# Four unread 64x64 products ahead of nine trains of matmuls in a two-block transformer on one core

## What is computed

```python
for l in range(DEPTH):                                   # DEPTH = 2
    h = rms_norm(x, norm_mix[l])
    if l < N_A:
        x = x + short_conv_mixer(h, conv_w_in[l], conv_w[l], conv_w_out[l])
    else:
        x = x + moba_attention(h, moba_w_q[j], moba_w_o[j], cos, sin, k_blk, v_blk, k_mean)
    x = x + mem_cross_attention(rms_norm(x, norm_mem[l]), rms_norm(mem, norm_memkv[l]),
                                mem_w_q[l], mem_w_kv[l], mem_w_o[l])
    x = x + swiglu(rms_norm(x, norm_ffn[l]), ffn_w_gu[l], ffn_w_down[l])
    if l == N_A - 1:
        k_blk, v_blk, k_mean = shared_kv(x, kv_norm, w_kv, cos, sin)
```

## Time and profile before

| what | value |
|---|---|
| median of 3 runs | 1797.46 us (1796.14 to 1797.94) |
| the profiled execution | 1793.09 us, its span 1791.3 us |
| busy share of the span | PE 89%, DVE 49%, ACT 37%, POOL 8% |
| chain that ended last | PE 62%, issue 28%, DVE 5%, ACT 3%, DMA 2% |
| matmuls of lines 422 to 424 | 1360 each, busy 379 us each line |

### The profile page before, as it was taken

One profiled execution on the slowest core, in us unless ns is written; L12 is line 12 of the kernel. 1 busy time (PEld: TensorE's weight loads), 2 busy tenths in 40 slices (PEclk: granted clock), 3 DMA queues, 4 the chain that ended last, 5 costly groups with the idle time before them and its releaser, 6 DMA issues.

```text
span 1791.3 us, 35143 instructions
## 1 busy us (share of the span) xinstructions
PE 1586.7 (89%) x14818; PEld 1313.8 (73%) x14818; DVE 869.1 (49%) x1231; ACT 665.6 (37%) x870; POOL 149.9 (8%) x188
## 2 busy tenths in 40 slices
PE   8999999999999999999999799799898676666677
PEld 8999899988979889988888699698884222222223
DVE  5865466646665555664667588956641000000001
ACT  5545355434544444533555744525431000000001
POOL 5900000000000000000105011131010000000000
PEclk9999999999999999999999899999998687786679
DMA  7755656765736657755453153002879999999997
GB/s 245 257 194 185 189 161 192 235 235 165 259 118 215 201 157 218 194 173 194 112 157 106 61 167 117 25 27 95 301 289 406 420 421 421 421 421 421 421 420 299
DMA packets 254141, 417.17 MB, mean 233 GB/s; under 512 B 15102, under 2 KB 215345, under 8 KB 229425
## 3 DMA queue, kind: packets, MB, share of 16 engines
q1 hardware_dynamic: 253825, 414.59, 64.8%
q10 hardware_dynamic: 176, 0.53, 0.1%
HBM read 414.04 MB, written 1.05 MB: 232 GB/s over the span
## 4 chain that ended last, share of the span: by engine, by line
PE 62%; issue 28%; DVE 5%; ACT 3%; DMA 2%; POOL 0%; DVEq 0%; SPq 0%; POOLq 0%; ACTq 0%
PE bank L422 8%; PE bank L423 8%; PE bank L424 8%; PE bank L438 4%; PE bank L439 4%; PE bank L440 4%; PE bank L1864 2%; PE bank L1063 2%; PE bank L1065 2%; PE bank L1064 2%; PE bank L747 2%; PE bank L839 1%; DMA w_raw<-in_ffn_w_gu_dram 1%; DVE cy L1413 1%; ACT w_hi L243 1%
## 5 line engine op out<-in xcount | busy, mean ns | idle before, releaser
L250 DVE TENSOR_TENSOR w_lo<-w_raw,w_hi 128x2048 fp32r<-128x2048 f32 (+2 forms) x178 | 401.8, 2260 | 252.9 <-ACT w_hi L243 252.8
L243 ACT ACTIVATE w_hi<-w_raw 128x2048 fp32r<-128x2048 f32 (+2 forms) x178 | 334.1, 1881 | 150.7 <-DMA w_raw<-in_ffn_w_down_dram 61.7
L422 PE MATMUL bank<-h_hi,w_hi 128*128 128x256 f32 x1168 | 325.5, 279 | 6.0 <-DVE h_lo L635 3.8
L424 PE MATMUL bank<-h_hi,w_lo 128*128 128x256 f32 x1168 | 324.6, 278 | 0.0
L423 PE MATMUL bank<-h_lo,w_hi 128*128 128x256 f32 x1168 | 324.5, 278 | 0.0
L2659 PE MATMUL bank<-w_exp,xeT 128*32 128x256 f32 x2048 | 172.2, 474 | 81.7 <-DMA w_exp<-in_w_up_dram 48.3
L422 PEld LDWEIGHTS bank<-h_hi,w_hi 128*128 128x128 f32 x1168 | 220.8, 189 | 7.4 <-issue 7.2
L424 PEld LDWEIGHTS bank<-h_hi,w_lo 128*128 128x128 f32 x1168 | 220.2, 189 | 0.0
L423 PEld LDWEIGHTS bank<-h_lo,w_hi 128*128 128x128 f32 x1168 | 220.1, 188 | 0.0
L2659 PEld LDWEIGHTS bank<-w_exp,xeT 128*32 128x32 f32 x2048 | 65.5, 128 | 182.7 <-DMA w_exp<-in_w_up_dram 83.9
L2659 PE MATMUL bank<-w_exp,hT 128*32 128x256 f32 x1024 | 97.1, 516 | 51.6 <-DMA w_exp<-in_w_down_dram 51.6
(11 more groups left out here) (537 smaller groups left out, 3102.1 us busy)
## 6 DMA issues: line engine op xcount, KB each, us to landing
w_exp<-in_w_gate_dram SPq DMA_DIRECT2D x64, 1024.0 KB, 27.0
w_exp<-in_w_up_dram SPq DMA_DIRECT2D x64, 1024.0 KB, 26.9
w_exp<-in_w_down_dram SPq DMA_DIRECT2D x64, 1024.0 KB, 27.0
w_raw<-in_ffn_w_gu_dram SPq DMA_DIRECT2D x88, 512.0 KB, 5.0
w_raw<-in_w_in_dram SPq DMA_DIRECT2D x54, 512.0 KB, 4.8
w_mod<-in_w_mod_dram SPq DMA_DIRECT2D x24, 1024.0 KB, 7.0
w_raw<-in_ffn_w_down_dram SPq DMA_DIRECT2D x44, 512.0 KB, 4.3
w_raw<-in_mem_w_kv_dram SPq DMA_DIRECT2D x32, 512.0 KB, 4.6
```

Of the source, the lines that this page charges most:

```text
L243: e.activation(whi[slot][:, 0:w], raw[slot][:, 0:w], ACT.Copy).then_inc(S["hi_ready"], 1)
L250: e.tensor_tensor(wlo[slot][:, 0:w], raw[slot][:, 0:w], whi[slot][:, 0:w].bitcast(F32), ALU.subtract).then_inc(S["lo_ready"], 1)
L422: e.matmul(dst, whi[slot][:, lo:hi_], bh[:, k, :], start=begin, stop=False)
L424: ins = e.matmul(dst, wlo[slot][:, lo:hi_], bh[:, k, :], start=False, stop=end)
```

## The change

`lead_in` writes four products of 64 x 64 by 64, two in the upper left and two in the lower right quarter of TensorE's array, from the identity into the bank that the train's chunk writes next. Nobody reads them: the chunk's first product starts that bank anew. `fm_chunk` gets a parameter `lead`, the number of the chunk ahead of which they stand. Seven calls set it, which makes nine trains, since two of the calls are made for both layers. It is chunk 0 for the last third of the conv input and the block-attention query, chunk 1 for the others.

```diff
+    def lead_in(e, dst):
+
+        for _ in range(2):
+            for a_ in (0, 64):
+                e.matmul(dst[a_:a_ + 64, 0:64], ident[a_:a_ + 64, a_:a_ + 64], ident[a_:a_ + 64, a_:a_ + 64],
+                         start=True, stop=True)
+
-    def fm_chunk(bh, bl, width=256, kts=KT):
+    def fm_chunk(bh, bl, width=256, kts=KT, lead=None):
 
         fs = width // P
 
         def chunk(e, c, u, slot):
             by_tile = st.tiles is not None
+            if isinstance(c, int) and c == lead:
+                lead_in(e, G[u])
...
-    gemm(4, cols(W), fm_chunk(h_hi, h_lo), act_chunk=copy_bc(0), ready=[th])
+    gemm(4, cols(W), fm_chunk(h_hi, h_lo, lead=1), act_chunk=copy_bc(0), ready=[th])
...
-    gemm(4, cols(W, first=2 * D), fm_chunk(h_hi, h_lo), dve_chunk=conv_chunk, dve_links=9,
+    gemm(4, cols(W, first=2 * D), fm_chunk(h_hi, h_lo, lead=0), dve_chunk=conv_chunk, dve_links=9,
          dve_ready=[t_bc, t_z0, t_vcol])
...
-    gemm(4, cols(A["mem_w_kv"][0]), fm_chunk(*h2), act_chunk=copy_fm(kT), ready=[t_memkv], act_ready=[t_conv_out],
+    gemm(4, cols(A["mem_w_kv"][0]), fm_chunk(*h2, lead=1), act_chunk=copy_fm(kT), ready=[t_memkv], act_ready=[t_conv_out],
...
-        gemm(4, cols(A["mem_w_q"][l]), fm_chunk(*into), act_chunk=copy_fm(qT), ready=[tx], act_ready=[tx],
+        gemm(4, cols(A["mem_w_q"][l]), fm_chunk(*into, lead=1), act_chunk=copy_fm(qT), ready=[tx], act_ready=[tx],
...
-        gemm(FT, source, fm_chunk(h_hi, h_lo), act_chunk=act_silu, dve_chunk=dve_gate, dve_links=2,
+        gemm(FT, source, fm_chunk(h_hi, h_lo, lead=1), act_chunk=act_silu, dve_chunk=dve_gate, dve_links=2,
...
-    gemm(4, cols(A["w_kv"]), fm_chunk(h_hi, h_lo), act_chunk=copy_fm(kT), ready=[th], act_ready=[th2])
+    gemm(4, cols(A["w_kv"]), fm_chunk(h_hi, h_lo, lead=1), act_chunk=copy_fm(kT), ready=[th], act_ready=[th2])
...
-    gemm(4, cols(A["moba_w_q"][0]), fm_chunk(*h2), act_chunk=copy_fm(qT), ready=[th2], act_ready=[t_memkv],
+    gemm(4, cols(A["moba_w_q"][0]), fm_chunk(*h2, lead=0), act_chunk=copy_fm(qT), ready=[th2], act_ready=[t_memkv],
```

## The result

Over ten executions each the changed kernel took 1803.09 us, the kernel before 1796.57: ratio 1.0037, with a 95% interval of 1.0023 to 1.0051. It is slower, by 6.5 us, where 1798.9 was forecast. Single executions of one kernel lie up to 13 us apart here (before: 1790.4 to 1803.4, where the three first ones lay within 1.8). I therefore timed the changed kernel twice more: 1.0016 (1.0001 to 1.0031) and 1.0024 (1.0003 to 1.0045). Taking the difference of the two means in each of these three timings, weighted by the inverse of its variance, gives **+4.2 us with a standard error of 0.7**, or 1.0024. The profiled execution took 1801.13 us with a span of 1799.3, 8.0 more than the span of before.

The account below looks back on a forecast made before the run. TensorE was taken as the bound wherever the change touches it, save at two places. The terms, 4 x 0.48 - 0.20 - 0.53 + 0.24 = +1.4 us, on timed runs of 1797.46 gave 1798.9, range 1793.8 to 1801.8.

Parts of the forecast that it names:

- six of six: All six line 452 trains behind 64x64 products, or transposes following them, were fast (276 ns, slow 281); basis for fast lead-ins.
- The price: Per lead-in on TensorE: 0.94 us from last matmul before to fourth behind, costing 0.48 in a fast train, 0.46 slow.
- Third conv-input: Lead-in in chunk 0: four slow chunks turn fast, 0.88 less for 0.46, but VectorE is the bound, so 0.
- Memory keys: Lead-in in chunk 1: some 0.27 delay hidden by TensorE's 1.26 us idle before the next chunk, so 0.
- Memory query of layer 0: Lead-in in chunk 1: three slow chunks left turn fast, 0.46 - 3 x 0.22 = -0.20 us.
- First feed-forward: Lead-in in chunk 1: train already fast throughout, so pure cost, +0.48 us.
- Block-attention query: Lead-in in chunk 0: four chunks and half a memory-keys chunk turn fast, 0.46 - 4.5 x 0.22 = -0.53 us.
- Second feed-forward: Lead-in in chunk 1: gain of chunks 2 to 5 lost in chunk 6's wait for weights, which lands later, +0.24 us.
- rival 1: Pace isn't set by what stands ahead, so lead-ins in all trains only cost: 3.3 us in all, 1800.8; chance 0.13.
- Rival 2: Timed runs hold more slow trains, which become fast: 1794.3 if the first feed-forward, 1791 with parts of the second; chance 0.17.
- Rival 3: Lead-ins make trains slow: first feed-forward +4.6 us on top of 3.3 for the products, 1805.4; chance 0.08.
- Rival 4: Gains at conv-input, memory keys and second feed-forward carried through, nothing swallowed: sum +0.4 us, 1797.9; chance 0.08.

Follow-up runs that it names:

- experiment 3: Changed kernel with the four products in the middle of every chunk of the nine trains, 64 places instead of nine: 1825.21 us, 1.0172 against the kernel before.
- experiment 5: The kernel before, unchanged, as a run of its own against itself: 1797.22 us, 1.0010.
- experiment 4: The changed kernel again with no edit, timed against the kernel before: 1797.82 us, 1.0016.
- experiment 1: Changed kernel with the lead-ins of the two feed-forwards taken out, the seven others kept: 1800.62 us, 1.0030 against the kernel before.
- experiment 2: Kernel before with lead-ins added in the two feed-forwards alone: 1797.38 us, 1.0015 against the kernel before.
- experiment 6: Kernel before with lead-ins only ahead of the third conv-input and block-attention query trains, in chunk 0: 1798.55 us, 1.0025 against the kernel before.

## Why the prediction was wrong, point by point

**The failing step** is "So I take it that a train is fast after its lead-in". Over all traces 99 groups of four 64x64 products stood in a running train with no wait ahead: FF 71, FS 0, SS 24, SF 4. A lead-in keeps the pace that it meets, but for one slow train in seven (53 of the 71 are from one trace, experiment 3). My six of six were trains of 24 matmuls in one execution, and the train ahead of the first of them, which has moving weights, was fast already; each of the others followed a fast one. So not one of the six had met a slow train:

```profile
L439 PE MATMUL bank<-w_lo,a_hi 128*128 128x256 f32 x15 | 4.1, 276 | 0.0
```

This is the stretch from 1080.3 to 1085.2 us in the profile that I worked from. The other traces hold what it lacked. In nine of the seventeen the train ahead of that first group is slow, and the train behind it is fast in all nine. In experiment 5, ahead of it (1089 to 1093.8 us), the group itself, and behind it (1095.2 to 1097.6):

```profile
L439 PE MATMUL bank<-w_lo,a_hi 128*128 128x256 f32 x14 | 3.9, 279 | 0.0
...
1093.83 1.15 PE L1864 MATMUL bank<-Tm,DR 64*64 64x64 f32 x32
...
L452 PE MATMUL bank<-h_hi,w_lo 128*128 128x256 f32 x7 | 1.9, 276 | 0.0
```

Over all seventeen traces the six trains are fast, 102 of 102. So what I had seen was real, but it is another sequence than the change's: sixteen or more products, two records to each, and a train with stationary weights behind one with moving weights. Two, four and eight products inside a train with stationary weights keep a slow pace in most cases. Whether the number of products or the change of form makes the difference, no run tries.

**The price** was mis-sized. I had 0.48 in a fast train and 0.46 in a slow one, from larger groups carried down to four products. Measured from the last matmul ahead to the fourth behind: 1.044 to 1.058, in 99 cases, in place of my 0.94. Less four intervals, a lead-in costs **0.59** (fast) or 0.58 (slow). The part that was short is from the first product to the first matmul, 0.37 in the timeline above (237.24 to 237.61) where I had 0.27. The cause is a misreading of the earlier trace rows: the x32 there are records, and each product in float32 leaves two of them, as the x8 of four products show. So the row is sixteen products (its loop in the kernel runs over eight by two), one costs 58 ns and not 29, and 1.08 - 24 records x 0.029 = 0.38 would have come out, and 0.60 for the lead-in. In the same way the four products span 0.23, not the 0.11 that I had named as their sign.

**The stage sums.**
- First conv-input, shared keys, memory query of layer 1: pure cost, as forecast, at 0.59 each.
- Third conv-input: turned fast as forecast. From the first of the transposes ahead of it to the start of the memory keys' third chunk, lead-in included, it takes 38.4 to 38.5 us in the five traces with products in that place and the next train's chunk 0 left alone, and 37.9 to 38.9 in seven without any there, 38.4 on average: no gain, as forecast. The profile that I worked from had 38.9, so against it the stage is 0.5 shorter.
- Memory keys: this lead-in comes behind a wait and the pace was drawn anew there (F to S in two of the three traces of the changed kernel); it was hidden as forecast.
- Memory query of layer 0: -0.20 forecast. In the traces its chunk 0 was fast already or stayed slow; +0.58 or 0.59.
- First feed-forward: I had it fast throughout. It was slow throughout, in all three traces of the changed kernel, and starts slow without products ahead of it in 10 of 13. Against the profile that I worked from this train is 5.2 us longer, 0.6 of it the lead-in; against the timed executions of before the pace adds little if they are as the 13 traces, since most of those have it as well.
- Block-attention query: -0.53 forecast; it was fast, with the lead-in dearer by 0.11, so -0.42 against a slow train. Without products it was slow in only 5 of 9, so -0.4 is the best case, and on average nothing is gained (0.57 - 5/9 x 0.99 = 0.0).
- Second feed-forward: +0.24 forecast. In the first trace it stayed slow up to chunk 6, where the wait went away and the train turned fast all the same. From the train's start to chunk 6 it took 34.6, before 35.0 with the wait, so the lead-in fell into that wait and cost 0. A wait longer than before, as I had written, was not there. Where it turned fast (experiment 4), chunk 6 began 33.7 behind the start. The landing isn't tied to the broadcasts as I had it: it varies by more than a microsecond between executions.

The first of the changed kernel's traces has these rows of TensorE around chunk 6. It begins at 708.41, 0.12 behind the last matmul of chunk 5, where it was 1.15 in the earlier trace rows:

```profile
708.29 0.28 PE L433 MATMUL bank<-h_hi,w_lo 128*128 128x256 f32 x1
708.41 0.35 PE L431 MATMUL bank<-h_hi,w_hi 128*128 128x256 f32 x1
708.60 0.28 PE L432 MATMUL bank<-h_lo,w_hi 128*128 128x256 f32 x1
```

**The sum by measured terms:** 0.59 three times, 0.58 for the memory query of layer 0, 0.58 for the first feed-forward, 0 for the block-attention query on average and 0 for the second feed-forward: +2.9 us, 1.0016. That is rival 1's mechanism in the main (its 3.3 had the lower price at seven places, where five pay). The three measurements give 4.2 +- 0.7. The 1.3 between them is 1.8 standard errors and stays open: chance, or a draw behind one of the later waits that the products' shift favours. Of the 6.5 us of the first measurement 3.6 are then unexplained. Nor do the times of the other runs follow the number of groups: by the means, seven groups (experiment 1) took 4.9 more than the kernel before, the two of experiment 2 2.7 and the two of experiment 6 3.4, each with a standard error of 1.1 to 1.2. What a lead-in costs is read from the traces; the times only agree with it roughly.

**The rivals.** Rival 1 (pace not set by what stands ahead) is what happened at seven of nine places, and failed at the two behind transposes. The Trainium skill's single warm spacing for 256 columns ("TensorE: Matmul & The Clock Gate", Back-to-back issue gap; it is given there for matmuls without their weight loads), which stood beside it, gave the right sign. Every trace here still has two spacings, 113.3 and 117.8 ns, both above its 109. Rival 2 had a premise that the further traces bear out, that other executions hold more slow trains than the profiled one, and a false conclusion, that lead-ins would turn them. Rival 3 was decided by the first feed-forward, and that was slow, 117.8 ns, in the first trace: read alone it would have confirmed rival 3 wrongly. The kernel before, run again, had the same slow train, and groups in 71 fast trains left them fast. Rival 4 assumed the gains.

**The range** ended at 1801.8 because I took three executions within 1.8 us for a steady kernel. With 29 of them the kernel before spreads over 13 to 17 us, and its medians over 10 to 29 executions go from 1792.9 to 1797.6.

## What to carry to other kernels

A difference of a few per cent between two stretches of the same instruction in one profile may be a state that is drawn anew at each wait: profile the unchanged kernel several times before an edit is built on it. Unread products in a running train are paid in full, here 0.59 us for four; the same ones inside a wait that is there anyway cost nothing. A rule taken from trains that always follow the same thing has to be looked at with both paces ahead of it before it carries a forecast: the six trains here had only met the fast one. And the x32 of a row counts records, which are not always instructions of the program: compare it with the loop that writes them.

## What the runs showed of the hardware

- A train of 128-row, 256-column matmuls with stationary weights runs at 113.3 or 117.8 ns, and holds this over a thousand matmuls (1008 in the first feed-forward of the changed kernel). Behind a wait either comes; between nominally equal executions the same train differs.
- Four 128-row products of 64 columns turn the pace, 62 of 64 and then 40 of 40 in the loops; four 64x64 ones keep it in 95 of 99. Behind sixteen 64x64 products a train with stationary weights was fast in 17 of 17, nine of them behind a slow train with moving weights. Why, no record shows: in both paces one weight load is issued per matmul, some 0.11 ahead of it. What the state is stays open.
- In FP32, four 64x64 products in two quadrants take 0.37 to the next matmul, four 128x64 ones 0.81, in two records each; those of the 128x64 ones lie mostly 0.11 apart for 64 columns, nearly as long as a train matmul takes for 256.
- In the first 600 us a stretch of 3.4 or 6.8 us at half clock (granted 0.50) comes at one place in one execution and at another in the next; up to 1330 us the seventeen traces have 27 to 48 us of it in all.
